# Pooled means without a scaling pass, and a new step order for projections, pool products and the output projection, in a two-block transformer kernel

## The reference

```
mod  = silu(c) @ w_ada + b_ada            # six rows of 1024: sh1 sc1 g1 sh2 sc2 g2
h    = rmsnorm(x) * (1 + sc1) + sh1
proj = h @ w_in                           # q (8 heads of 64), k, v (2 heads), u_pool (4 groups of 128)
att  = softmax(q k^T / 8) v               # q and k normed and rotated
for group g, window w in (2, 4, 8, 16):   # lo = max(t - w/2, 0), hi = min(t + w/2 - 1, 511)
    pooled_g = sum(u_g[lo..hi]) / (hi - lo + 1) - u_g[t]
    pool_g   = (pooled_g @ w_pool[g]) * pool_scale
x    = x + g1 * (concat(att, pool) @ w_out)
h2   = rmsnorm(x) * (1 + sc2) + sh2       # then a gated feed-forward, then the second block
```

## Time and profile before

| | |
|---|---|
| median of 3 runs | 1401.18 us (1401.03 to 1401.99) |
| the profiled execution | 1401.18 us, its span 1399.4 us |
| PE busy | 1357.0 us (97%) |
| DVE busy | 763.4 us (55%) |
| POOL busy | 710.9 us (51%) |
| ACT busy | 632.9 us (45%) |
| mean granted TensorE clock | 0.987 of full speed |

### The profile page before, as it was taken

The page is one execution under the profiler, slowest core; times in us unless marked ns, Lnnn a source line. Parts: engine busy times, 40 slices in busy tenths (PEclk is TensorE's granted clock), DMA queues, the critical chain, the costliest instruction groups (busy, mean ns, idle before and its releaser), DMA issues.

```text
span 1399.4 us, 17597 instructions
## 1 busy us (share of the span) xinstructions
PE 1357.0 (97%) x7007; PEld 1117.3 (80%) x7007; DVE 763.4 (55%) x1249; ACT 632.9 (45%) x1170; POOL 710.9 (51%) x386
## 2 busy tenths in 40 slices
PE   7799899999999999999999999999999999999998
PEld 7676489888888888897777777778888888888886
DVE  5578955776677574556776755325185421312224
ACT  4546635444431441635777755555554332313321
POOL 1248852655564454554333654348607654645560
PEclk8799999999999999999999999999999999999999
DMA  8424561555555554411122121124302222222321
GB/s 332 148 68 140 156 216 61 184 191 196 211 180 191 194 190 139 143 62 62 60 81 70 61 91 60 35 87 151 120 1 83 96 92 90 91 93 93 115 91 60
DMA packets 32050, 167.54 MB, mean 120 GB/s; under 512 B 3552, under 2 KB 4192, under 8 KB 18912
## 3 DMA queue, kind: packets, MB, share of 16 engines
q1 hardware_dynamic: 31968, 166.42, 34.6%
HBM read 164.31 MB, written 2.10 MB: 119 GB/s over the span
## 4 chain that ended last, share of the span: by engine, by line
PE 86%; DVE 7%; ACT 3%; DMA 2%; issue 1%; POOL 1%; SPq 0%; DVEq 0%; ACTq 0%
PE B L549 82%; DMA ZF<-in_w_ada_rows 2%; DVE ZF L1868 1%; PE B L969 1%; ACT WH L1190 1%; PE B L793 1%; POOL WL L2297 1%; DVE ST L1968 1%; DMA RAW<-in_x 1%; DVE SC L1951 0%; DVE SC L1946 0%; DVE SC L1766 0%; PE B L697 0%; DVE ZF L1859 0%; DVE SC L1782 0%
## 5 line engine op out<-in xcount | busy, mean ns | idle before, releaser
L2297 POOL TENSOR_TENSOR WL<-RAW,WH 128x512 fp32r<-128x512 f32 (+1 forms) x203 | 466.2, 2311 | 467.8 <-ACT WH L1190 423.2
L549 PE MATMUL B<-HH,WH 128*128 128x512 f32 (+2 forms) x1040 | 403.8, 391 | 3.9 <-ACT HH L1272 2.1
L549 PE MATMUL B<-HH,WL 128*128 128x512 f32 (+2 forms) x1040 | 396.6, 384 | 0.0
L549 PE MATMUL B<-HL,WH 128*128 128x512 f32 (+2 forms) x1040 | 385.3, 382 | 0.0
L1190 ACT ACTIVATE WH<-RAW 128x512 fp32r<-128x512 f32 (+1 forms) x203 | 192.8, 980 | 194.6 <-PE B L549 178.3
L549 PEld LDWEIGHTS B<-HH,WH 128*128 128x128 f32 x1040 | 196.3, 189 | 44.5 <-issue 5.3
L549 PEld LDWEIGHTS B<-HH,WL 128*128 128x128 f32 x1040 | 196.2, 189 | 38.9
L549 PEld LDWEIGHTS B<-HL,WH 128*128 128x128 f32 x1040 | 191.4, 188 | 34.5
L549 PE MATMUL B<-ZR,WH 128*128 128x512 f32 (+1 forms) x624 | 164.7, 352 | 0.7 <-POOL WL L2297 0.7
L2309 POOL TENSOR_TENSOR ZR<-SC,ZR 128x512 fp32r<-128x512 f32 (+1 forms) x72 | 97.9, 1362 | 115.1 <-ACT ZR L1682 50.8
L1868 DVE CUSTOM_DVE_ANT_0 ZF<-ZF,VT 128x1024 f32<-128x1024 f32 x80 | 134.1, 1703 | 19.7 <-DMA ZF<-in_w_ada_rows 19.5
(11 more groups left out here) (247 smaller groups left out, 1789.6 us busy)
## 6 DMA issues: line engine op xcount, KB each, us to landing
RAW<-in_slabs SPq DMA_DIRECT2D x102, 1024.0 KB, 4.9
ZF<-in_w_ada_rows SPq DMA_DIRECT2D x80, 512.0 KB, 4.3
G<-in_w_ada SPq DMA_DIRECT2D x8, 512.0 KB, 10.2
RAW<-in_slabs SPq DMA_DIRECT2D x4, 768.0 KB, 4.4
RAW<-in_x SPq DMA_DIRECT2D x4, 512.0 KB, 6.2
SC<-in_w_ada SPq DMA_DIRECT2D x4, 512.0 KB, 9.2
ZF<-in_w_ada SPq DMA_DIRECT2D x4, 512.0 KB, 10.0
out<-SC SPq DMA_DIRECT2D x8, 256.0 KB, 2.1
```

The source lines that it names most:

```text
L549: return e.matmul(out, l, r, start=start, stop=stop)
L2297: e.tensor_tensor(lo[:, at], k.RAW[:, i % 2, at], hi[:, at].bitcast(F32), ALU.subtract).then_inc(*w.hit((i, q)))
```

## The change

The scaling by 1/w on GpSimd is left out. Instead ScalarE's copy into `PA` scales by 1/w, so that the window sums are already the means, and a second copy from PSUM puts the unscaled group into `MEAN[g]`, from which the last step subtracts in place. The edge columns are multiplied in the window sum's own place by count corrections, which are `EDGE` times w. `MEAN[3]` is another buffer. The tables move: p0 to p3 start one or two steps earlier, the pool products two to four steps earlier, the first half of the output projection is done at steps 28, 29, 32 and 34, and the modulation tiles from the seventh on one step earlier.

```diff
@@ constants
+    edge *= np.array([2, 4, 8, 16], np.float32)[:, None]
@@ the tables
-ADA1 = [*range(9, 22, 2), *range(22, 39)]
-
-T1 = {"q3": 0, "p0": 5, "p1": 10, "p2": 15, "p3": 20}
-
-POOL_OUT = {24: 0, 26: 1, 28: 2, 30: 3}
+ADA1 = [*range(9, 20, 2), *range(20, 38)]
+
+T1 = {"q3": 0, "p0": 4, "p1": 9, "p2": 13, "p3": 18}
+
+POOL_OUT = {22: 0, 23: 1, 24: 2, 26: 3}
+
+MIX = {28: 0, 29: 1, 32: 2, 34: 3}
@@ buffers
-        self.MEAN = [G[:, 2560 + 512 * i:3072 + 512 * i] for i in range(3)] + [self.PB[:, 16:528]]
+        self.MEAN = [G[:, 2560 + 512 * i:3072 + 512 * i] for i in range(3)] + [self.slot(0)]
@@ pe_program
-        if 32 <= s < 36:
-            mix(s - 32, 0, 4, ("main", "main", "s", "s")[s - 32])
+        if s in MIX:
+            mix(MIX[s], 0, 4, ("main", "main", "s", "s")[MIX[s]])
@@ act_program
-                e.activation(k.PA[:, 16:528], B[x][:, :], ACT.Copy).then_inc(*mix.hit(("pa", g)))
-                B.free(x, mix["pa", g])
+                e.activation(k.PA[:, 16:528], B[x][:, :], ACT.Copy, scale=1.0 / (2, 4, 8, 16)[g]).then_inc(
+                    *mix.hit(("pa", g)))
+                e.activation(k.MEAN[g], B[x][:, :], ACT.Copy).then_inc(*mix.hit(("px", g)))
+                B.free(x, mix["px", g])
@@ pool_program, mean_ops
-        pool.wait_ge(mix["win", g, w])
-        e.tensor_scalar(other[:, 16:528], src[:, 16:528], 1.0 / w, None, ALU.mult).then_inc(*mix.hit(("part", g)))
-        yield
         for c0, e0 in ((0, 0), (504, 8)):
-            pool.wait_ge(mix["part", g])
-            e.tensor_tensor(other[:, 16 + c0:24 + c0], src[:, 16 + c0:24 + c0], k.EDGE[:, 16 * g + e0:16 * g + e0 + 8],
+            pool.wait_ge(mix["win", g, w])
+            e.tensor_tensor(src[:, 16 + c0:24 + c0], src[:, 16 + c0:24 + c0], k.EDGE[:, 16 * g + e0:16 * g + e0 + 8],
                             ALU.mult).then_inc(*mix.hit(("edge", g, c0)))
         yield
         pool.wait_ge(mix["edge", g, 504])
-        e.tensor_tensor(m, other[:, 16:528], PA[:, 16:528], ALU.subtract).then_inc(*mix.hit(("mean", g)))
+        pool.wait_ge(a_mix["px", g])
+        e.tensor_tensor(m, src[:, 16:528], m, ALU.subtract).then_inc(*mix.hit(("mean", g)))
```

## The result

The changed kernel takes 1408.76 us (median of 4 runs, 1407.53 to 1409.92) against 1401.46 us before (4 runs): a ratio of 1.0051, 95% interval 1.0037 to 1.0066. It is slower by 7 us, where 1403.3 us and at most 1407 were forecast. The profiled execution took 1407.91 us with a span of 1406.1 us.

What follows compares the result with a forecast made beforehand. The prediction held the stage's end paced by VectorE's progress plus loads' round trips, not TensorE's work. Shift of pair 3's product +2.4 and norm -0.3 gave +2.1 on 1401.2: 1403.3 us; 8-in-10 range 1398.5 to 1407.

Steps and rivals of the forecast that it cites:

- S: Shift of pair 3's product on VectorE, taken equal to VectorE's shift at step 30: +2.4 us, bounds -1.1 to +4.5.
- Step 22 at 142.0: TensorE's score of step 22 moves from 140.63 to 142.0 us, from one quarter of a projection at 1.42 us.
- One falls into the early gaps: Of two earlier projection quarters, one costs nothing, filling TensorE's gaps of 3.1 us before 120 us.
- Mean at 158.0: GpSimd's fourth pooled mean, needed at step 26, ends at 158.0 us, between 155.7 and 158.5; TensorE waits 4.2 us.
- Restart 0.9 us for the clock: TensorE's lower clock after the step 26 pause adds 0.9 us before step 28's score; bounds 0 and 1.8.
- VectorE gives back 0.7: After step 30's maxima, VectorE finds loads landed and GpSimd calmer, recovering 0.7 us, between nothing and 1.0.
- held longer at step 26: Rival: mean at 158.5, no slow tile given back, lower clock for the whole restart and again later; 1406.3 us, chance 0.22.
- VectorE relieved: Rival: fewer GpSimd instructions return VectorE's slow tiles of steps 24 to 29 to 1.29 us; 1399.8 us, chance 0.22.
- The gaps are filled: Rival: tail tied to TensorE, so 7.7 us of gaps from 148 to 198 and 1.8 of clock go; 1391.7 us, chance 0.10.

Runs made afterwards that it cites:

- e4: Changed kernel with p0 and p1 back at steps 5 and 10, p2 at 14 and p3 still at 18: 1406.22 us.
- e5: Changed kernel's order with the old arithmetic: GpSimd scales again and ScalarE's second copy is gone; 1410.58 us.
- e8: Kernel before with the new arithmetic, pool products at steps 24, 25, 26, 28 and mixes at 30, 31, 32, 34; projections and tiles unmoved: 1400.97 us.
- e10: New arithmetic, early pool products and mixes, old projections and tiles, plus ScalarE's second slab split moved behind norm 2's first-half root: 1398.88 us, 0.9979 against before.
- e1: Changed kernel with the modulation tiles back in their old steps: 1408.55 us.
- e11: Kernel before with only ScalarE's split of the second 1 MB slab moved behind the root of norm 2's first half: 1400.91 us.
- e2: Changed kernel with the fourth pool product at step 28 instead of 26 and the first two mixes at 30 and 31: 1405.33 us.
- e9: Changed kernel with p0, p1, p2 at steps 5, 10, 14, the fourth pool product at 28 and the first mixes at 30 and 31: 1403.26 us.

## Why the prediction was wrong

The mechanism that was forecast is there: step 20 later by the quarters of a projection, TensorE held in step 26 by the fourth mean, VectorE's maxima late, the tail tied to it, the norm held by a slab's landing (ScalarE's split waits for it at 211.53 us, though it is the first of the two slabs of 1 MB and not, as was forecast, the second). Two signs did not come as stated: TensorE's wait for the mean is 2.93 us and not 4.2, as 2.64 us of exponentials now stand ahead of it, and between 198 and 206 us TensorE is idle for 2.5 us, not 3 to 5. The step that failed is in the sum for S, the shift of pair 3's product (2.4 us forecast, 6.8 measured): its first term, in which one of the two earlier quarters was to vanish in TensorE's early gaps at no cost. Term by term:

- **Step 22 at 142.0; measured 145.12.** +3.1 us, the largest miss. "One falls into the early gaps" was wrong. Nothing was saved by it: e4 shows both quarters (2.84 us by the rows) as 2.74, where 1.42 was forecast, and the early p0 and p1 add 1.6 where they were to cost nothing. The early gaps of TensorE are waits for VectorE and ScalarE, and the one that was filled, in step 6, opened again in steps 8 to 18. A part of it is ScalarE's second copy, for which the forecast allowed at most 0.6 us once per group and put nothing in the sum: without it (e5) step 20 comes 0.65 us earlier.
- **Mean at 158.0; measured 162.6.** Of this 3.1 us are step 22's. Pair 1's subtraction came 3.76 us after step 22, as worked out (3.9). From there 13.7 us were needed for the 12.1 that I took, 12.6 being the upper end: the four window sums took 7.4 instead of 5.6 us. Behind the earlier trace rows one of the four was long (1.95 us, the others 1.08 to 1.30); after the change three were (1.95, 2.08 and 2.18). +1.5 us. The range's end was no upper bound.
- **Restart 0.9 us for the clock; measured 1.8.** From the mean's end to the score of step 28 it took 5.3 us (162.60 to 167.87) where 3.5 + 0.9 were forecast; the granted clock of 148 to 174 us fell to 0.87. +0.9 us. This was the upper end of the forecast's own bounds (0 and 1.8).
- **VectorE gives back 0.7; measured 1.8.** From the maxima of step 30 to the product it is 20.4 us, before 22.1. −1.1 us.

Together 3.1 + 1.5 + 0.9 − 1.1 = 4.4, and 2.4 + 4.4 = 6.8. The norm gave back 1.4 of this instead of 0.3, and the clock at 1040 us cost 1.2 in this execution, which no term of the forecast has: 1401.2 + 5.4 + 1.2 = 1407.8, against 1407.9 measured. Without it this execution would have ended at 1406.7 us, inside the range; that the median, 1408.76, holds it too isn't shown.

The rival "held longer at step 26" named the right place and the right sign, and its 1406.3 us was still too low, for the same first step. "VectorE relieved" fell: the ten tiles from 148 to 184 us took 1.78 us on average, as in the earlier trace rows, although four scalings were gone. "The gaps are filled" fell wholly; e8 does the pool products and the first mixes earlier, in those gaps, and gains nothing.

The rule that the prediction weighed (the Trainium skill, SBUF — State Buffer, "SBUF: two separate sides") was used for VectorE alone. By the same rule GpSimd is held by VectorE's tiles: its window sums took 1.08 us or up to 2.18, and its subtractions 1.26 or 2.24. The trace agrees. Costed at the longer length throughout, four sums at 2.07 (the mean of the three long ones) give 8.3 us instead of 5.6, 2.7 us more, where the chain as a whole was missed by 1.6.

What stays open is how the 1.6 us of the early p0 and p1 divide among ScalarE's copies ahead of the exponentials, the wait for VectorE in step 8, and VectorE's order of maxima, rotations and tile. Only the second copy was tried (0.65 us, in e5, with the scaling changed as well), and p2 and p3 were not tried alone.

## What to carry to other kernels

Work moved earlier into a gap isn't free. In this kernel the gap was a round trip through other engines, so price moved work in full and credit a gap only where the trace shows which engine is waited for and that it doesn't wait for you in turn. Look also at what the moved work drags along: here a copy changed places with exponentials in another engine's queue. Before making a product earlier, find the last operand and add up its whole chain at the disturbed length of each instruction, not at the mean of a lucky row. And where two chains of nearly the same length end in one place (VectorE's tiles and TensorE's products here), shortening one shows in the trace and not in the time: e10's gain came from taking a slab's split out of the chain that both feed.

## What the runs showed of the hardware that wasn't expected

- A norm sum that the change doesn't touch lost 1.2 us at 1040 us in three of thirteen profiles (after, e1 and e11; e11 differs from before only in the place of one split). In after the granted clock fell to 0.57 for 4 us behind waits of 0.94 and 0.80 us on ScalarE; in before the same waits, 0.94 and 0.79 us, left it at 1.00. A shift of all the work ahead of it is enough to bring it or not.
- The same holds for longer waits. Behind the wait for the norm's first sum the clock fell in e2 (1.90 us), e4 (2.27) and e5 (1.86) and cost 1.5 us each, and stayed full in e9 (2.02).
- Behind that norm a profile's shift against before stays what it is up to its end, to 0.15 us in nine of the twelve; the three that lose 1.1 to 1.3 us more are those with the fall at 1040 us.
- The time up to the first score of the loop differed by 2.2 us between profiles (78.85 to 81.08), in code that all of them share. Comparisons of single profiles by absolute times carry this difference; counted from that score, step 20 repeated to 0.03 us among the kernels with the same `T1` and tiles (55.89 to 55.92).
